# Linear attention's opening pass: TensorE turns the decayed keys ahead of the modulation chunk's matmuls, state sums ahead of the chunk's group sum

## The chip, the cores and the metric

One NeuronCore of a Trainium2 chip runs the whole program. The metric is the device time in microseconds (us) of one execution; the number given for a kernel is the median of its runs. The engines are TensorE (PE; PEld is its weight load), VectorE (DVE), ScalarE (ACT), GpSimd (POOL) and SyncE (SP), which here only issues DMA transfers. Each engine works through its own instructions in the order in which they are written, and a wait on a semaphore at the head of an engine's queue holds everything behind it on that engine.

## The reference

The program computes one transformer layer for 128 context tokens and 1024 latent tokens. Two parts of it meet in the stretch that is changed. The first is the linear attention (4 heads, keys of 64 and values of 128), in chunks with a decay that depends on the data:

```
def step(S, xs):
    qc, kc, vc, gc = xs
    cum = jnp.cumsum(gc, axis=2)
    o_inter = jnp.einsum('bhik,bhkv->bhiv', qc * jnp.exp(cum), S)
...
    last = cum[:, :, -1:, :]
    S = (jnp.exp(last[:, :, 0, :])[..., None] * S
         + jnp.einsum('bhjk,bhjv->bhkv', kc * jnp.exp(last - cum), vc))
```

It runs once forward and once backward over the tokens. The second is the modulation, a vector of 6 x 1024 numbers for each of the two conditioning vectors:

```
m = (jax.nn.silu(cond) @ w_ada + b_ada)[:, None, :]
sh1, sc1, g1, sh2, sc2, g2 = jnp.split(m, 6, axis=-1)
h = rms_norm(x, norm_mix) * (1 + sc1) + sh1
...
x = x + g1 * mo
h = rms_norm(x, norm_ffn) * (1 + sc2) + sh2
x = x + g2 * moe_ffn(h, *ffn_p)
```

Only `sh1` and `sc1` are needed before the token mixer. The other four parts, 4096 columns of `w_ada`, are computed beside the linear attention. Attention, the output projection and a mixture of 32 experts follow.

## The kernel before

The program is a row of stages (`with stage(...)`), written with an explicit queue for each engine and explicit semaphores. A stage ends with all engines meeting before the next begins. The changed code is in the second stage, which holds the linear attention. In the trace of before it runs from about 358 us to about 478 us.

There are nine tiles of 128 tokens (`NT` = 9: one of context, eight latent), taken in the order of `FIRST` in an opening pass, and in the order of `SECOND` in a closing pass that makes the outputs. The opening pass is one loop on every engine, with `i` from 0 to 8. For tile i:

- PE `gates(i)` (L920, 4 products) makes the gate's pre-activations, five tiles ahead.
- ACT `size` (L704, L705) and `log` (L709) turn them into logarithms of decays. `log` needs another function table, so an ACT_TABLE_LOAD stands ahead of each block of `log`, and another ahead of the next `grow`. Two `size` come after `grow(0)` and `grow(3)`; one `size` and three `log` come after `grow(1)` and `grow(4)`.
- DVE `decay(i)` (L819 to L833) scans them into cumulated decays.
- ACT `grow(i)` (L716, L718, L719) takes exponentials; its first instruction, L716, makes `ek`.
- DVE `decay_keys(i)` (L838) multiplies the keys with `ek` and signals `kf_made`.
- PE `turn(i)` (L929) transposes the decayed keys into PSUM bank 2. ACT `keep_turned(i)` (L724) copies them out as `kTM` and signals `kTM_made`.
- PE `sums(i)` (L939) multiplies them with the values: the tile's contribution to the state. DVE `add(i)` (L844) scales it, and `step` (L854) carries the states from tile to tile.

Mixed into the same loop, for `i` from 0 to 7 (`NADA` = 8), is one chunk of 512 modulation columns:

- SP `load(n)` (L657) fetches 2 MB of `w_ada` into one of two buffers `RING_B`. From chunk 2 on it waits for `ada_parted` of chunk n-2, which used the buffer. `row_out(n-2)` (L670) and `rows(n)` (L662) follow on SP, and wait for `mod2_ready`. For n = 5, SP also waits for the fifth `mod2_ready` before it reloads `nrow2` (L666); `load(6)` is queued behind that.
- PE `ada_part(n)` (L949) makes four groups of partial products in PSUM bank 6, and ACT `ada_keep(n)` (L732) copies them to SBUF and signals `part_kept`.
- PE `ada_sum(n)` (L957) adds the groups and the bias into bank 7. ACT `ada_row(n)` (L740) copies out the row and signals `mod2_ready`; for n = 4 and 5, DVE `ada_scaled(n)` (L861) does so in its place.

On ACT the loop's body is, in this order, `grow(i)`, any `size` and `log`, the three copies, and then `grow(i+1)`. On DVE it is `decay(i+1)`, `decay_keys(i)`, `add(i-1)`, `step(i-3)`, and `ada_scaled(i-1)` for the two chunks named. After the loop DVE goes through `mask(0)`, the last `add` and the remaining `step`, and then the closing pass.

Of the kernel before, what the change touches and what calls it, by code (L numbers as in the profile page):

```python
# [36 lines left out]
def trunk_kernel(nc, t_in, t_out):  # L37
# [52 lines left out]
    with ctx:  # L90
# [5 lines left out]
        def sem(name):  # L96
            if name not in sems:
                sems[name] = nc.alloc_semaphore(name=f"{name}_{stages[0]}")
            return sems[name]
# [183 lines left out]
        def bank(b, n=H, off=0):  # L283
            return PS[:, b * H + off:b * H + off + n]
# [346 lines left out]
        NADA = 8  # L631
# [11 lines left out]
        with stage("pads_out cache_in") as block:  # L643
# [54 lines left out]
            @block.scalar  # L698
            def _(act):
                own = Chain(act, sem("own_gla_act"))  # L700

                def size(i):
                    act.wait_ge(sem("z_made"), i + 1)
                    own.link(nc.scalar.activation(u4(ag[i]), u4(bank(z_bank(i))), ACT.Abs))  # L704
                    nc.scalar.activation(ag[i], ag[i], ACT.Exp, scale=-1.0).then_inc(sem("z_exp"), 1)  # L705

                def log(i):
                    act.wait_ge(sem("z_exp"), i + 1)
                    nc.scalar.activation(ag[i], ag[i], ACT.Ln, bias=1.0).then_inc(sem("ln_made"), 1)  # L709

                def grow(i):
                    g = FIRST[i]
                    act.wait_ge(sem("decay_made"), i + 1)
                    if i >= 2:
                        act.wait_ge(sem("kf_made"), i - 1)
                    nc.scalar.activation(ek[i % 2], Dt[i % 2], ACT.Exp, scale=-1.0 / 16).then_inc(sem("ek_made"), 1)  # L716
                    act.wait_ge(sem("qf_made"), i)
                    nc.scalar.activation(eq, Dt[i % 2], ACT.Exp, scale=1.0 / 16).then_inc(sem("eq_made"), 1)  # L718
                    nc.scalar.activation(vecs[:, :, :, g], vecs[:, :, :, g], ACT.Exp, scale=1.0 / 16).then_inc(sem("vecs_made"), 1)  # L719

                def keep_turned(i):
                    act.wait_ge(sem("kf_turned"), i + 1)
                    act.wait_ge(sem("sums_made"), i)
                    nc.scalar.activation(kTM, bank(2), ACT.Copy).then_inc(sem("kTM_made"), 1)  # L724

                def ada_keep(n):
                    act.wait_ge(sem("ada_parted"), n + 1)
                    if n >= 2:
                        act.wait_ge(sem("ada_summed"), n - 1)
                    else:  # L730
                        act.wait_ge(sem("part2_cleared"), 1)
                    nc.scalar.activation(part2[n % 2][0:BIAS_ROW], bank(6)[0:BIAS_ROW], ACT.Copy).then_inc(sem("part_kept"), 1)  # L732

                def ada_row(n):
                    if n in (4, 5):
                        return
                    act.wait_ge(sem("ada_summed"), n + 1)
                    if n >= 2:
                        act.wait_ge(sem(f"rows_out{n % 2}"), 16 * (n // 2))
                    nc.scalar.activation(mrow2[n % 2], bank(7)[0:2, :], ACT.Copy).then_inc(sem("mod2_ready"), 1)  # L740

                def square(s):
                    act.wait_ge(sem("gla_made"), s + 1)
                    act.wait_ge(sem("o_mean"), s)
                    for h in range(GH):
                        last = nc.scalar.activation(osq[:, h * P:(h + 1) * P], bank(o_bank(s) + h % 2, P, h // 2 * P), ACT.Square, accum_out=so4[:, h:h + 1])
                    last.then_inc(sem("o_squared"), 1)

                for i in range(3):
                    size(i)  # L750
                for i in range(3):
                    log(i)
                for i in range(NT):
                    grow(i)
                    if i + 3 < NT and i % 3 == 0:
                        size(i + 3)
                        size(i + 4)
                    if i + 4 < NT and i % 3 == 1:
                        size(i + 4)
                        for k in range(i + 2, i + 5):  # L760
                            log(k)
                    if i < NADA:
                        ada_keep(i)
                    keep_turned(i)
                    if i < NADA:
                        ada_row(i)
                for s in range(NT):
                    square(s)
# [143 lines left out]
            def _(pe):  # L912
                pe.wait_ge(sem("gate_w_in"), 64)

                def gates(i):
                    g = FIRST[i]
                    if i >= 4:
                        pe.wait_ge(sem("decay_logged"), i - 3)
                    for u in range(4):
                        last = nc.tensor.matmul(bank(z_bank(i), P, u * P), WG[u // 2][:, (u % 2) * P:(u % 2 + 1) * P], lrT1[:, g * P:(g + 1) * P],  # L920
                                                start=True, stop=True)
                    last.then_inc(sem("z_made"), 1)

                def turn(i):
                    g = FIRST[i]
                    pe.wait_ge(sem("kf_made"), i + 1)
                    pe.wait_ge(sem("kTM_made"), i)
                    for u in range(4):
                        last = nc.tensor.transpose(bank(2, P, u * P), kf[:, g, u * P:(u + 1) * P], ident)  # L929
                    last.then_inc(sem("kf_turned"), 1)  # L930

                def sums(i):
                    g = FIRST[i]
                    pe.wait_ge(sem("kTM_made"), i + 1)
                    pe.wait_ge(sem("added"), i)
                    for u in range(4):
                        for half in range(2):
                            h = 2 * (u % 2) + half
                            last = nc.tensor.matmul(bank(3, P, u * P)[64 * half:64 * half + 64], kTM[:, u * P + 64 * half:u * P + 64 * half + 64],  # L939
                                                    v_all[:, g, h * DV:(h + 1) * DV], start=True, stop=True)  # L940
                    last.then_inc(sem("sums_made"), 1)

                def ada_part(n):
                    pe.wait_ge(sem(f"ada2_in{n % 2}"), 16 * (n // 2 + 1))
                    pe.wait_ge(sem("part_kept"), n)
                    for jj in range(2):
                        for r in range(4):
                            j = 2 * r + jj
                            last = nc.tensor.matmul(bank(6)[32 * r:32 * r + 32], scP[:, j * 32:(j + 1) * 32], RING_B[n % 2][:, j, :],  # L949
                                                    start=(jj == 0), stop=(jj == 1))  # L950
                    last.then_inc(sem("ada_parted"), 1)

                def ada_sum(n):
                    pe.wait_ge(sem("part_kept"), n + 1)
                    pe.wait_ge(sem(f"brow2_in{n % 2}"), 16 * (n // 2 + 1))
                    pe.wait_ge(sem("mod2_ready"), n)
                    nc.tensor.matmul(bank(7)[0:2, :], sel, part2[n % 2], start=True, stop=True).then_inc(sem("ada_summed"), 1)  # L957

                def score(s):
                    g = SECOND[s]  # L960
                    pe.wait_ge(sem("qf_made"), FIRST.index(g) + 1)
                    pe.wait_ge(sem("gla_masked"), 2 * s)
                    for u in range(4):
                        for half in range(2):
                            rows = slice(64 * half, 64 * half + 64)
                            last = nc.tensor.matmul(bank(half, P, u * P), kf[rows, g, u * P:(u + 1) * P], qkT[rows, u, g * P:(g + 1) * P],
                                                    start=True, stop=True)
                    last.then_inc(sem("gla_scored"), 1)
# [25 lines left out]
                for i in range(NT):  # L994
                    if i + 5 < NT:
                        gates(i + 5)
                    if i < NADA:
                        ada_part(i)
                    if i == NT - 1:
                        score(0)  # L1000
                    turn(i)
                    if i < NADA:
                        ada_sum(i)
                    sums(i)
                for s in range(NT):
                    if s + 1 < NT:
                        score(s + 1)
# [1164 lines left out]
```

## Time and profile before

| | before |
|---|---|
| runs, us | 2623.21, 2623.43, 2631.17 |
| median, us | 2623.43 |
| profiled execution: time, us | 2625.44 |
| profiled execution: span, us | 2623.8 |
| PE busy | 2393.7 us, 91% |
| DVE busy | 1545.6 us, 59% |
| ACT busy | 1337.5 us, 51% |
| granted TensorE clock, mean | 0.965 |

The span is the time from the first to the last instruction of the profiled execution, and the execution's own time is 1.6 us longer. The busy shares are those of the whole program, most of which is the mixture of experts. For a change in a single stage the rows of that stage are to be read, by time. A granted clock of 1.00 is TensorE at 2.4 GHz, and 0.50 is 1.2 GHz.

### The profile page before, as it was taken

The numbers are of one execution on the slowest core, as the hardware profiler recorded it, in microseconds if no ns is written. First come the engines' busy times: TensorE is split into PE (matmuls) and PEld (weight loads), VectorE is DVE, ScalarE is ACT, GpSimd is POOL, SyncE is SP. The second block draws the span as 40 slices with busy tenths as digits, with TensorE's granted clock in tenths as the row PEclk, the third lists the DMA queues.
The fourth block names the chain that finished last, engine by engine and source line by source line (L and its number), as shares of the span: only waits on it lengthen the run. The fifth ranks groups of instructions, "written<-read, shape, count | busy, mean of one in ns | idle before, by whom it ended". The sixth has DMA issues, their size and how long they took to land.

```text
span 2623.8 us, 55140 instructions
## 1 busy us (share of the span) xinstructions
PE 2393.7 (91%) x19125; PEld 1346.1 (51%) x19126; DVE 1545.6 (59%) x1828; ACT 1337.5 (51%) x1395; POOL 831.7 (32%) x946
## 2 busy tenths in 40 slices
PE   6999987799989959899899998889988999999991
PEld 2555555577755535455455554445544555545550
DVE  2222247566636675953934659999689624175975
ACT  1111143366532345843834658888588524165861
POOL 1222223500003353433333443434334433233322
PEclk9999989999999979999999999999999999999995
DMA  8000043420032286964945869999899835177974
GB/s 322 21 18 18 9 155 124 136 81 0 0 130 82 99 291 221 396 237 130 362 169 164 284 240 361 398 396 394 292 343 397 300 87 169 28 276 264 359 278 177
DMA packets 180248, 538.48 MB, mean 205 GB/s; under 512 B 20672, under 2 KB 37490, under 8 KB 180142
## 3 DMA queue, kind: packets, MB, share of 16 engines
q1 hardware_dynamic: 150620, 487.79, 49.0%
q0 software_dynamic: 26656, 46.85, 8.1%
q10 hardware_dynamic: 2916, 3.14, 0.4%
q8 instruction: 30, 0.49, 0.1%
q14 instruction: 26, 0.21, 0.0%
HBM read 493.11 MB, written 45.20 MB: 205 GB/s over the span
## 4 chain that ended last, share of the span: by engine, by line
PE 55%; DVE 6%; issue 5%; DMA 2%; ACT 2%; POOL 0%; ACTq 0%; DVEq 0%; POOLq 0%; SPq 0%
PE psum L2065 44%; PE psum L1968 5%; DVE arena L1836 4%; PE psum L2054 2%; PE psum L2049 2%; DMA arena<-in_w_down 1%; PE psum L2043 1%; ACT arena L1657 1%; PE psum L1984 1%; DMA expert_lists<-arena 0%; DVE arena L1930 0%; DVE arena L1931 0%; PE psum L1977 0%; DVE arena L1944 0%; DVE arena L1895 0%
## 5 line engine op out<-in xcount | busy, mean ns | idle before, releaser
L2065 PE MATMUL psum<-arena 128*64 128x512 bf16 x12528 | 1422.9, 383 | 66.6 <-DVE arena L1885 36.0
L2065 PEld LDWEIGHTS psum<-arena 128*64 128x64 bf16 x12528 | 717.5, 111 | 721.8 <-DVE arena L1836 49.6
L1836 DVE TENSOR_TENSOR arena<-arena 128x2048 bf16<-128x2048 f32 x384 | 862.7, 2287 | 184.9 <-ACT arena L1657 177.9
L1657 ACT ACTIVATE arena<-arena 128x2048 bf16<-128x2048 f32 x384 | 723.2, 1904 | 94.9 <-DVE arena L1836 64.9
L1566 POOL DMA_INDIRECT expert_sums<-arena x90 | 185.7, 2064 | 671.6 <-issue 649.7
L555 PE MATMUL psum<-arena 128*128 128x512 f32 (+2 forms) x864 | 298.9, 505 | 1.1 <-ACT arena L411 1.1
L555 PEld LDWEIGHTS psum<-arena 128*128 128x128 f32 x864 | 151.0, 191 | 133.6 <-issue 129.0
L1885 DVE TENSOR_TENSOR arena<-psum,arena 128x512 bf16<-128x512 f32 x87 | 59.8, 688 | 234.3 <-ACT arena L1699 234.3
L1537 POOL DMA_INDIRECT arena<-expert_inputs,arena x88 | 108.2, 1230 | 198.4 <-PE psum L2043 178.5
L1695 ACT ACTIVATE arena<-psum 128x1024 bf16<-128x1024 bf16 x87 | 88.5, 1017 | 156.4 <-issue 153.8
L1710 ACT ACTIVATE arena<-psum,arena 128x512 f32<-128x512 f32 x87 | 59.3, 681 | 201.0 <-PE psum L2065 201.0
L1968 PE MATMUL psum<-arena 128*128 128x512 f32 x288 | 129.7, 605 | 1.4 <-DVE arena L1766 1.4
L1699 ACT ACTIVATE arena<-psum 128x512 bf16<-128x512 f32 x87 | 51.5, 592 | 155.8 <-PE psum L2049 155.6
L1895 DVE TENSOR_SCALAR arena<-psum 128x512 f32<-128x512 f32 x87 | 59.8, 687 | 111.1 <-PE psum L2065 111.1
L1588 POOL COPY arena<-arena 128x2 int32<-128x2 int32 x86 | 124.7, 1450 | 0.0
L1575 POOL DMA_DIRECT2D arena<-expert_lists x172 | 97.7, 585 | 51.7 <-issue 50.7
L1126 ACT ACTIVATE arena<-psum 128x512 f32<-128x512 f32 x104 | 58.0, 595 | 97.5 <-PE psum L1256 97.5
L2054 PE MATMUL psum<-arena 128*64 128x512 bf16 x522 | 103.1, 391 | 3.9 <-issue 3.4
L1256 PE MATMUL psum<-arena 128*128 128x128 f32 x640 | 92.1, 283 | 13.1 <-ACT arena L1126 8.2
L1553 POOL COPY arena<-arena 128x6 f32<-128x6 f32 x90 | 76.0, 845 | 83.6 <-DMA expert_sums<-arena 83.6
L1155 DVE TENSOR_REDUCE arena<-psum 128x1 f32<-128x512 f32 (+1 forms) x96 | 54.7, 599 | 64.2 <-PE psum L1219 64.2
L1106 ACT ACTIVATE arena<-psum,arena 128x1280 f32<-128x1280 f32 x64 | 84.9, 1327 | 7.2 <-DVE arena L1159 1.7
(268 smaller groups left out, 2161.5 us busy)
## 6 DMA issues: line engine op xcount, KB each, us to landing
arena<-in_w_gu SPq DMA_DIRECT2D x256, 1024.0 KB, 18.4
arena<-in_w_down SPq DMA_DIRECT2D x128, 1024.0 KB
arena<-in_w_ada SPq DMA_DIRECT2D x12, 2048.0 KB, 9.0
arena<-in_x_sample SPq DMA_DIRECT2D x16, 512.0 KB, 3.6
arena<-in_w_in SPq DMA_DIRECT2D x3, 2048.0 KB, 19.6
expert_sums<-arena SPq DMA_DIRECT2D x10, 512.0 KB, 6.1
expert_inputs<-arena SPq DMA_DIRECT2D x10, 512.0 KB, 2.8
x_after_mixing<-arena SPq DMA_DIRECT2D x9, 512.0 KB, 2.7
```

The costliest lines, as they stand in the source:

```text
L555: last = nc.tensor.matmul(bank(bk, n, off), hT[b][:, j * P:(j + 1) * P], w_in[:, j, lo:lo + n], start=(j == 0), stop=(j == KT - 1))
L1256: last = nc.tensor.transpose(bank(t_bank(r - 1, i), P, at * P), pr[(r - 1) % 2][:, v * KEYS + k * P:v * KEYS + (k + 1) * P], ident)
L1537: pool.indirect_dma_start(out=xg, out_offset=None, in_=h2_d, in_offset=bass.IndirectOffsetOnAxis(ap=present.bitcast(U32)[:, 0:1], axis=0)) ...
L1566: pool.indirect_dma_start(out=moe_halves, out_offset=bass.IndirectOffsetOnAxis(ap=held.bitcast(U32)[:, 2 * DELAY:2 * DELAY + 1], axis=0), ...
L1575: pool.dma_start(listed[group(h), :], pairs[:, h, :]).then_inc(sem("listed_in"), 16)
L1588: nc.gpsimd.tensor_copy(present, listed).then_inc(sem("present_kept"), 1)
L1657: nc.scalar.activation(high(e, p, c), raw[p][c], ACT.Copy).then_inc(sem(f"hi_made{c}"), 1)
L1695: nc.scalar.activation(xT, bank(B_X).bitcast(BF), ACT.Copy).then_inc(sem("xT_made"), 1)
L1836: nc.vector.tensor_tensor(w_lo[p][c], raw[p][c], high(e, p, c), ALU.subtract).then_inc(sem(f"lo_made{c}"), 1)
L1968: last = nc.tensor.matmul(bank(a), mixT[b][:, j * P:(j + 1) * P], w_out[:, j, a * H:(a + 1) * H], start=(j == 0), stop=(j == KT - 1))
L2054: nc.tensor.matmul(bank(b)[group(g)], pickrow[:, (first + g) * UNIT:(first + g + 1) * UNIT], rows, start=True, stop=False)
L2065: last = nc.tensor.matmul(bank(b)[group(g)], parts[part][:, cols], w[:, kk, g * H:(g + 1) * H], start=False, stop=(k == KT - 1 and part == 1))
```

## The change

Two pairs of calls change places in PE's loop, and one pair on ACT. On PE, `turn(i)` now stands ahead of `ada_part(i)`, and `sums(i)` ahead of `ada_sum(i)`. On ACT, `keep_turned(i)` stands ahead of `ada_keep(i)`. No instruction is added or removed, and no wait is changed.

```diff
@@ -759,10 +759,9 @@
                         size(i + 4)
                         for k in range(i + 2, i + 5):
                             log(k)
+                    keep_turned(i)
                     if i < NADA:
                         ada_keep(i)
-                    keep_turned(i)
-                    if i < NADA:
                         ada_row(i)
                 for s in range(NT):
                     square(s)
@@ -994,14 +993,14 @@
                 for i in range(NT):
                     if i + 5 < NT:
                         gates(i + 5)
-                    if i < NADA:
-                        ada_part(i)
                     if i == NT - 1:
                         score(0)
                     turn(i)
                     if i < NADA:
+                        ada_part(i)
+                    sums(i)
+                    if i < NADA:
                         ada_sum(i)
-                    sums(i)
                 for s in range(NT):
                     if s + 1 < NT:
                         score(s + 1)
```

On PE, in the iteration i = 2 of the opening pass, the rows of before read as follows. L920 is `gates`, L949 `ada_part`, L929 `turn`, L957 `ada_sum` and L939 `sums`; the brackets hold the semaphores that the instruction waits for, and `kf_made` comes from DVE's `decay_keys`.

```order
L920 MATMUL psum<-arena 128x128 [waits decay_logged_1]
L920 MATMUL psum<-arena 128x128 x3
L949 MATMUL psum<-arena 32x512 [waits part_kept_1,ada2_in0_1]
L949 MATMUL psum<-arena 32x512 x7
L929 MATMUL psum<-arena 128x128 [waits kTM_made_1,kf_made_1]
L929 MATMUL psum<-arena 128x128 x3
L957 MATMUL psum<-arena 2x512 [waits mod2_ready_1,brow2_in0_1,part_kept_1]
L939 MATMUL psum<-arena 64x128 [waits added_1,kTM_made_1]
L939 MATMUL psum<-arena 64x128 x7
```

In the change the same iteration reads as follows. The line numbers of PE's functions are one lower there: L928 is `turn`, L948 `ada_part`, L938 `sums` and L956 `ada_sum`.

```order
L919 MATMUL psum<-arena 128x128 [waits decay_logged_1]
L919 MATMUL psum<-arena 128x128 x3
L928 MATMUL psum<-arena 128x128 [waits kTM_made_1,kf_made_1]
L928 MATMUL psum<-arena 128x128 x3
L948 MATMUL psum<-arena 32x512 [waits part_kept_1,ada2_in0_1]
L948 MATMUL psum<-arena 32x512 x7
L938 MATMUL psum<-arena 64x128 [waits added_1,kTM_made_1]
L938 MATMUL psum<-arena 64x128 x7
L956 MATMUL psum<-arena 2x512 [waits mod2_ready_1,brow2_in0_1,part_kept_1]
```

The wait for `kf_made` now stands ahead of the eight products of `ada_part`, and `ada_sum` is the last of the iteration.

On ACT, the end of the same iteration and the start of the next read as follows before. L732 is `ada_keep`, L724 `keep_turned`, L740 `ada_row`, and L716 the first instruction of the next `grow`.

```order
L732 ACTIVATE arena<-psum 98x512 [waits ada_summed_1,ada_parted_1]
L724 ACTIVATE arena<-psum 128x512 [waits sums_made_1,kf_turned_1]
L740 ACTIVATE arena<-psum 2x512 [waits rows_out0_1,ada_summed_1]
L716 ACTIVATE arena<-arena 128x512 [waits kf_made_1,decay_made_1]
L718 ACTIVATE arena<-arena 128x512 [waits qf_made_1]
```

In the change they read:

```order
L724 ACTIVATE arena<-psum 128x512 [waits sums_made_1,kf_turned_1]
L732 ACTIVATE arena<-psum 98x512 [waits ada_summed_1,ada_parted_1]
L740 ACTIVATE arena<-psum 2x512 [waits rows_out0_1,ada_summed_1]
L716 ACTIVATE arena<-arena 128x512 [waits kf_made_1,decay_made_1]
L718 ACTIVATE arena<-arena 128x512 [waits qf_made_1]
```

The two copies have changed places; the row's copy L740 still stands ahead of the next `grow`, and still waits for `ada_sum`.

## Rows read from the trace of the kernel before

**Rows 1.** The page's chain that ended last, by line, share of the span.

```profile
PE psum L2065 44%; PE psum L1968 5%; DVE arena L1836 4%; PE psum L2054 2%; PE psum L2049 2%; DMA arena<-in_w_down 1%; PE psum L2043 1%; ACT arena L1657 1%; PE psum L1984 1%; DMA expert_lists<-arena 0%; DVE arena L1930 0%; DVE arena L1931 0%; PE psum L1977 0%; DVE arena L1944 0%; DVE arena L1895 0%
```

**Rows 2.** Windows: us, PE, PEld, DVE, ACT, POOL busy (x), PEclk, DMA share, GB/s.

```profile
372.40:428.00 55.60, 44.63 (x331) 18.62 (x332) 41.81 (x104) 34.90 (x65) 12.48 (x16) 0.87 0.74 262
428.07:438.50 10.43, 8.81 (x106) 7.73 (x106) 10.39 (x28) 2.35 (x11) 2.77 (x4) 1.00 0.00 0
```

**Rows 3.** Timeline of DVE: start, duration; all of `decay_keys` but i = 6.

```profile
373.04 0.68 DVE L838 TENSOR_TENSOR arena<-arena 128x512 f32<-128x512 f32 x1
...
378.93 0.69 DVE L838 TENSOR_TENSOR arena<-arena 128x512 f32<-128x512 f32 x1 [1.26 <-ACT arena L716]
...
387.80 0.69 DVE L838 TENSOR_TENSOR arena<-arena 128x512 f32<-128x512 f32 x1 [1.59 <-ACT arena L716]
...
392.78 0.68 DVE L838 TENSOR_TENSOR arena<-arena 128x512 f32<-128x512 f32 x1
...
398.69 0.69 DVE L838 TENSOR_TENSOR arena<-arena 128x512 f32<-128x512 f32 x1
...
405.44 0.69 DVE L838 TENSOR_TENSOR arena<-arena 128x512 f32<-128x512 f32 x1 [0.39 <-ACT arena L716]
...
423.46 0.69 DVE L838 TENSOR_TENSOR arena<-arena 128x512 f32<-128x512 f32 x1 [4.96 <-ACT arena L716]
...
428.07 0.69 DVE L838 TENSOR_TENSOR arena<-arena 128x512 f32<-128x512 f32 x1 [2.08 <-ACT arena L716]
```

**Rows 4.** Timeline of PE, iteration i = 2.

```profile
386.16 1.16 PE L920 MATMUL psum<-arena 33*128 33x128 f32 x8
387.24 1.92 PE L949 MATMUL psum<-arena 128*32 128x512 f32 x16
389.10 0.66 PE L929 MATMUL psum<-arena 128*128 128x128 f32 x4
389.88 1.02 PE L957 MATMUL psum<-arena 128*2 128x512 f32 x2
390.83 1.09 PE L939 MATMUL psum<-arena 128*64 128x128 f32 x16
```

**Rows 5.** Timeline of ACT, end of iteration i = 2.

```profile
389.23 0.60 ACT L732 ACTIVATE arena<-psum 98x512 f32<-98x512 f32 x1 [0.83 <-PE psum L949]
...
390.94 0.59 ACT L740 ACTIVATE arena<-psum 2x512 f32<-2x512 f32 x1 [0.55 <-PE psum L957]
391.43 0.61 ACT L716 ACTIVATE arena<-arena 128x512 f32<-128x512 f32 x1
```

**Rows 6.** Timeline of PE: the waits of i = 1, 4 and 6.

```profile
384.18 1.02 PE L957 MATMUL psum<-arena 128*2 128x512 f32 x2 [1.88 <-ACT arena L732]
...
403.03 1.29 PE L957 MATMUL psum<-arena 128*2 128x512 f32 x2 [2.40 <-ACT arena L732]
404.26 1.98 PE L939 MATMUL psum<-arena 128*64 128x128 f32 x16
...
416.91 3.64 PE L949 MATMUL psum<-arena 128*32 128x512 f32 x16 [5.63 <-DMA arena<-in_w_ada]
```

**Rows 7.** Timeline of ACT: around the blocks of `log`, i = 1 and 4.

```profile
383.56 0.57 ACT L732 ACTIVATE arena<-psum 98x512 f32<-98x512 f32 x1
...
385.84 1.28 ACT L716 ACT_TABLE_LOAD   x1
...
397.13 0.61 ACT L716 ACTIVATE arena<-arena 128x512 f32<-128x512 f32 x1
...
404.78 0.63 ACT L716 ACTIVATE arena<-arena 128x512 f32<-128x512 f32 x1
```

**Rows 8.** Timeline of DVE and of SP: `ada_scaled(4)`, and the issue of `load(6)`.

```profile
407.89 0.67 DVE L861 SCALAR_TENSOR_TENSOR arena<-psum,arena 2x512 f32<-2x512 f32 x1
...
408.87 0.39 SPq L657 DMA_DIRECT2D arena<-in_w_ada  x1
```

**Rows 9.** Windows, with the granted clock: behind the waits of 1.88 and 2.40 us.

```profile
382.00:385.00 3.00, 1.12 (x5) 0.15 (x3) 2.29 (x3) 2.62 (x5) 0.00 (x0) 1.00 1.00 313
403.00:406.00 3.00, 2.97 (x18) 1.66 (x18) 2.54 (x10) 2.97 (x5) 0.00 (x0) 0.61 0.04 14
```

## Prediction

> **What bounds the kernel now.** I read the page's chain first: over half of the span hangs on the experts' matmuls, which the change doesn't touch [rows 1]. So its worth has to be read from the stage of the linear attention, and passed on one to one: all engines meet at the stage's end, and nothing of the next stage starts ahead of that.
>
> The windows come next. In the opening pass, 55.60 us long, PE is busy for 44.63, DVE for 41.81 and ACT for 34.90: no engine is full, so the pass is held by chains between them. In the 10.43 us behind it DVE is busy for 10.39 [rows 2]. That stretch is one unbroken run of DVE from `decay_keys(8)` to its last `step`, and the closing pass hangs on it. **So what the change does to the time is what it does to the start of `decay_keys(8)`.**
>
> The timeline of DVE gives the beat of the pass, the starts of `decay_keys` [rows 3]. From i = 0 to 5 the steps are 5.89, 8.87, 4.98, 5.91 and 6.75 us, from i = 5 to 7 it is 18.02, and from 7 to 8 it is 4.61. Where a row of it has a wait, it is for ACT's L716, the exponential.
>
> What sets the beat before? Chunk i's row is a loop of its own: `ada_part(i)`, `ada_sum(i)`, ACT `ada_row(i)`, the next `grow`, `decay_keys(i+1)`. But `ada_part(i+1)` doesn't wait for `decay_keys(i+1)`; it runs while ACT and DVE make the keys. In iteration 2, `ada_part` runs from 387.24 to 389.16, and `decay_keys(2)` from 387.80 to 388.49: the keys are ready before `turn` gets to them, and cost PE nothing [rows 3, 4].
>
> PE has three waits of note: 1.88 and 2.40 us for ACT's copy in iterations 1 and 4, where ACT is still at its `log`, and 5.63 us for `load(6)` [rows 6]. That load is issued at 408.87, right behind `ada_scaled(4)`, which ends at 408.56, and its data let PE go at 416.91, 8.04 us later [rows 6, 8].
>
> **The change part by part.** It moves work and adds none: 8 `ada_part`, 9 `turn`, 9 `sums`, 8 `ada_sum`, 17 copies. SP's list stays as it is, with its waits; what it waits for moves.
>
> *What is won.* The three waits above are partly filled: `sums` now covers the wait for `ada_keep`, `ada_part` that for `keep_turned`. This gives PE room, but the beat isn't set by PE's room.
>
> *What is lost.* `turn(i)` waits for `decay_keys(i)`, and now `ada_part(i)` is behind it. `ada_sum(i)` is behind `sums(i)`, and ACT's next `grow` still waits for `ada_row(i)`, which waits for `ada_sum(i)`. The two loops close into one: keys, turn, part, sums, group sum, row, exponential, keys. At full clock, start to start or with a handover of 0.05 us (L716 to L732 show such):
> - `decay_keys` 0.68 and a handover 0.05: 0.73 [rows 3]
> - `turn` 0.66 [rows 4]
> - `ada_part` 387.24 to 389.10: 1.86 [rows 4]
> - `sums` 1.09, taken as 1.04 to the next start; `ada_sum` 1.02 and a handover: 1.06 [rows 4]
> - `ada_row` 390.94 to 391.43: 0.49; L716 0.61 and a handover: 0.66 [rows 5]
>
> That is 6.50 us. Now each step against [rows 3]:
> - **2 to 3:** 6.50 for 4.98, +1.5.
> - **3 to 4:** 6.50, and 0.25 since two `size` of 1.15 us each hold up `keep_turned(3)` until just after `ada_part(3)`. 6.75 for 5.91, +0.8.
> - **7 to 8:** 6.50 for 4.61, +1.9.
> - **0 to 1:** PE is at half clock when it begins. `ada_part` takes 3.64 there, as a slow one does [rows 6], in place of 1.86: 8.3 for 5.89, +2.4. If the clock rises within that `ada_part` it is +1.3; if `sums` is slow as well (1.98 [rows 6]), +3.3.
> - **1 to 2:** ACT's `log` sets it. Its copies can start at 383.56 as before [rows 7]; now `keep_turned` is first (0.60 and a handover), then come `sums` 1.04, `ada_sum` 1.06, `ada_row` 0.49, the table 1.28 [rows 7], and L716 0.66. That leads to 388.74 in place of 387.80: +0.9.
> - **4 to 5:** ACT alone sets it, from `grow(4)` at 397.13 to `grow(5)` at 404.78, 7.65 us [rows 7], since no `ada_row(4)` is on ACT. Before, `decay_keys(4)` came late by DVE's own work and the step was 6.75: +0.9.
> - **5 to 7:** `load(6)` is issued 3.43 us after `decay_keys(5)` starts, on DVE's work alone, and takes its 8.04 [rows 3, 6, 8]. From `ada_part(6)` to `decay_keys(7)` it was 6.55 [rows 3, 6]; now it is 3.57 at half clock, and 1.04, 1.06, 0.49, 0.66: 6.8. +0.3, or +1.1 with a slow `sums`. The wait of 5.63 doesn't absorb what was lost earlier, as the load's issue is late by the same amount.
>
> The sum is 1.5 + 0.8 + 1.9 + 2.4 + 0.9 + 0.9 + 0.3 = **+8.7 us** at full clock in the middle of the pass.
>
> *The clock.* PE now idles ahead of nearly each `turn`. From the end of `ada_sum(i-1)` it is 0.05 + 0.49 + 0.66 + 0.73, 1.9 us, to `turn(i)`: all of it idle in iterations 4, 6 and 7, less 1.1 us of `gates` [rows 4] in 1 to 3, and 1.28 more for the table in iteration 2, 2.1 us. The rows of before bound what such a wait does: behind 1.88 us the granted clock was 1.00, behind 2.40 us it was 0.61, and the next `sums` took 1.98 instead of 1.09 [rows 4, 6, 9]. The new waits of about 2 us lie in between. An iteration at half clock costs 3.64 - 1.92 in `ada_part` and 1.98 - 1.09 in `sums`, 2.6 us, where the loop sets the step (2 to 3, 3 to 4, 7 to 8). I take one half of one such iteration, 1.3 us: **+10.0 us.** The Trainium skill, in "TensorE: Matmul & The Clock Gate", section "A second HAM failure mode: psum-queue depth-cycling", tells of a kernel whose short idle times between groups of matmuls make the clock go back and forth between its two levels. By that rule all three of these iterations would be slow, and the sum would be that of the second rival below; the trace so far agrees only for the wait of 2.40 us.
>
> **The rivals.**
> 1. *The loop closes through `ada_part`* (the forecast): +8 to +13 us. Chance 0.65.
> 2. *The same, and the clock stays down.* The three steps lose 2.6 us each, 0 to 1 is at its 3.3, 5 to 7 at its 1.1: 8.7 + 7.8 + 0.9 + 0.8 = +18 us. Against it: PE is busy for more of a slow iteration than of a fast one, and in before the granted clock had a mean of 0.87 over the pass with its waits of 2.40 and 5.63 us in it [rows 2, 6]. Chance 0.12, from +13 up.
> 3. *The pass is held by the modulation weights, and early losses vanish in PE's wait for `load(6)`* (no change). For it: 5.63 us of wait, the longest in the pass. Then only what comes behind counts, 0.3 + 1.9 = +2 us. It decides if `ada_scaled(4)` isn't late, that is if `decay_keys(5)` isn't. Against it: the steps to there add up to 6.5. A partial form, in which the clock rises early and some steps lose less, ends near +7. Chance 0.20 for both.
> 4. *Faster: the room on PE is what counts.* If ACT's next `grow` gained from the earlier `keep_turned`, and PE's waits of 1.88, 2.40 and 5.63 us all vanished, the pass would be 9.9 us shorter. It takes a `grow` that isn't behind `ada_row`; the order on ACT speaks against it. Chance 0.03.
>
> **How the numbers follow.** The profiled span of 2623.8 would become 2633.8, and its own time of 2625.44 would be 2635.4; the median lies 2.0 below that time, so 2623.43 + 10.0 = 2633.4. From no change a measurement here tells about 0.3%, 7.9 us (2631.3). The forecast and rival 2 lie above that, rival 3 below, rival 4 at the other side: slower 0.77, same 0.20, faster 0.03. The range for 8 in 10 goes from +6 (the partial form of rival 3) to +16.5 (most of rival 2): 2629.5 to 2640.
>
> **What would show it.** In the trace after, PE's `turn` should have waits for DVE's keys in iterations 0 to 7, of 1 to 2 us, and no wait for ACT's `ada_keep`. The beat of `decay_keys` should be 6.5 us from 2 to 3 and from 7 to 8. `load(6)` should be issued some 6.5 to 9 us later than 408.87, and PE should still wait for it, some 3 us. `decay_keys(8)` should start near 438, and the rest of the program keep its lengths. I am wrong if `ada_part` comes through at its old times although it is behind `turn`, or if the later stages shift by more than the pass; and wrong in size if the clock takes another way than above.

## The result and the profile after

The changed kernel takes 2641.52 us (median of 6 runs, 2639.14 to 2647.64), beside 2626.76 us for the kernel before (6 runs, 2623.21 to 2631.17). The ratio is 1.0061, with a 95% interval of 1.0049 to 1.0072: slower by 13 to 19 us. Timed again on another occasion (the run `after_again`) it was 2642.29 us beside 2628.24 us, a ratio of 1.0040 (1.0025 to 1.0056), or 7 to 15 us. The ratios are estimates with intervals of their own; the plain quotients of the medians are 1.0056 and 1.0053, inside both. The forecast was 2633.4 us, in a range of 2629.5 to 2640.0: the direction was right, and the time lies above the range.

The beat of the pass comes first, as in [rows 3]. In the changed kernel `decay_keys` has line L837. These are rows of DVE's timeline (start, duration, operation, and in brackets the idle time ahead and what ended it):

```profile
376.06 0.68 DVE L837 TENSOR_TENSOR arena<-arena 128x512 f32<-128x512 f32 x1
385.00 0.69 DVE L837 TENSOR_TENSOR arena<-arena 128x512 f32<-128x512 f32 x1 [4.32 <-ACT arena L716]
394.89 0.69 DVE L837 TENSOR_TENSOR arena<-arena 128x512 f32<-128x512 f32 x1 [2.63 <-ACT arena L716]
402.94 0.69 DVE L837 TENSOR_TENSOR arena<-arena 128x512 f32<-128x512 f32 x1 [2.98 <-ACT arena L716]
409.58 0.69 DVE L837 TENSOR_TENSOR arena<-arena 128x512 f32<-128x512 f32 x1 [0.65 <-ACT arena L716]
417.24 0.69 DVE L837 TENSOR_TENSOR arena<-arena 128x512 f32<-128x512 f32 x1 [0.39 <-ACT arena L716]
423.74 0.68 DVE L837 TENSOR_TENSOR arena<-arena 128x512 f32<-128x512 f32 x1
435.94 0.69 DVE L837 TENSOR_TENSOR arena<-arena 128x512 f32<-128x512 f32 x1 [5.63 <-ACT arena L716]
443.98 0.69 DVE L837 TENSOR_TENSOR arena<-arena 128x512 f32<-128x512 f32 x1 [5.52 <-ACT arena L716]
```

From the first to the ninth it is 67.92 us, where it was 55.03 us in [rows 3]: **+12.9 us**. Below, "the pass" always means this stretch. DVE now waits for ACT's exponential in seven of the nine rows, twice for over 5 us.

What follows the pass kept its lengths. From the ninth `decay_keys` to TensorE's first instruction of the next stage it is 50.14 us (50.13 before), and from there to the end of the span 2145.5 us (2145.6). What lies ahead did not: the stage begins 2.9 us later than in the trace of before, at 360.91 instead of 358.05, in code that the change doesn't touch. 12.9 and 2.9 are the 15.8 us between the two spans, 2639.6 and 2623.8.

Iteration 2 on TensorE, beside [rows 4]; L928 is `turn`, L948 `ada_part`, L938 `sums`, L956 `ada_sum`:

```profile
395.64 0.95 PE L928 MATMUL psum<-arena 128*128 128x128 f32 x4 [2.26 <-DVE arena L837]
396.52 3.26 PE L948 MATMUL psum<-arena 128*32 128x512 f32 x16
399.72 1.09 PE L938 MATMUL psum<-arena 128*64 128x128 f32 x16
400.74 1.02 PE L956 MATMUL psum<-arena 128*2 128x512 f32 x2
```

And ACT in the same iteration, beside [rows 5], with SyncE's issue of `load(6)`, beside [rows 8]:

```profile
399.86 0.60 ACT L732 ACTIVATE arena<-psum 98x512 f32<-98x512 f32 x1 [2.63 <-PE psum L948]
401.80 0.59 ACT L740 ACTIVATE arena<-psum 2x512 f32<-2x512 f32 x1 [1.34 <-PE psum L956]
...
420.66 0.39 SPq L657 DMA_DIRECT2D arena<-in_w_ada  x1
```

The reader is to see the order of time. `decay_keys(2)` starts at 394.89; `turn` waits for it; `ada_part`, `sums` and `ada_sum` follow in one block; ACT's row copy waits for `ada_sum` at 401.80; and `decay_keys(3)` starts at 402.94. One thing is behind the other all the way round. `ada_part` takes 3.26 us where it took 1.92 [rows 4], since the clock fell right behind the wait of 2.26 us. The windows show it (us, PE, PEld, DVE, ACT and POOL busy, granted clock, DMA share, GB/s): iteration 2 from `turn` to the end of `ada_part`, and the wait and the work of iteration 7. The clock is still 1.00 while TensorE waits, and 0.56 in the work behind.

```profile
395.60:399.70 4.10, 4.06 (x20) 1.15 (x20) 4.00 (x9) 0.60 (x1) 1.46 (x2) 0.58 0.22 53
434.00:436.60 2.60, 0.76 (x2) 0.00 (x0) 0.66 (x2) 1.74 (x4) 0.00 (x0) 1.00 0.02 4
437.00:440.70 3.70, 3.70 (x20) 0.90 (x18) 1.45 (x3) 0.60 (x1) 1.23 (x2) 0.56 0.00 0
```

### The profile page after: what moved, and what is told of

Its sections match the earlier page's. It is cut to its first block, busy times and chain, and to the rows that moved or that the text cites. A ratio compares the mean times of both kernels' runs of the same rounds, so it can differ in the third digit from the quotient of the medians.

```text
span 2639.6 us, 55140 instructions
## 1 busy us (share of the span) xinstructions
PE 2396.2 (91%) x19125; PEld 1344.7 (51%) x19126; DVE 1546.0 (59%) x1828; ACT 1337.6 (51%) x1395; POOL 833.6 (32%) x946
## 4 chain that ended last, share of the span: by engine, by line
PE 53%; DVE 6%; issue 5%; DMA 3%; ACT 2%; POOL 1%; ACTq 0%; DVEq 0%; SPq 0%; POOLq 0%
PE psum L2064 42%; PE psum L1967 5%; DVE arena L1835 4%; DMA arena<-in_w_down 2%; PE psum L2053 2%; PE psum L2048 2%; PE psum L2042 1%; ACT arena L1656 1%; PE psum L1983 1%; DVE arena L1929 0%; DMA expert_lists<-arena 0%; DVE arena L1894 0%; DVE arena L1930 0%; PE psum L1976 0%; DVE arena L1943 0%
```

## The experiments

Theory A is that of the prediction, with the clock as the miss in size. The rivals that were tried against it: B, all of the loss is the place of `sums`; C, all of it is `turn`'s wait ahead of `ada_part`; D, the clock is the larger part of the loss, or, for the long steps, none of it. Each kernel's pass is read from its own trace.

| kernel | pass, us | steps 2 to 3 / 5 to 7 / 7 to 8, us | ratio to before (95%) |
|---|---|---|---|
| before; again | 55.03; 54.84 | 4.98 / 18.02 / 4.61 | |
| change; again | 67.92; 68.97 | 8.05 / 18.70 / 8.04 | 1.0061; 1.0040 |
| `e9_scalar_only` | 62.35 | 5.32 / 19.36 / 5.66 | 1.0043 (1.0027 to 1.0059) |
| `e1_turn_only` | 63.21 | 7.42 / 17.97 / 6.17 | 1.0034 (1.0023 to 1.0044) |
| `e2_sums_only` | 64.50 | 5.31 / 19.46 / 5.31 | 1.0043 (1.0028 to 1.0057) |
| `e3_row_later` | 55.60 | 4.99 / 16.17 / 5.33 | 0.9998 (0.9989 to 1.0006) |
| `e4_filled` | 77.89 | 10.20 / 25.42 / 8.74 | 1.0097 (1.0082 to 1.0111) |
| `e5_filled_less` | 64.48 | 8.64 / 16.46 / 6.41 | 1.0035 (1.0023 to 1.0048) |
| `e6_before_load6` | 49.43 | 4.99 / 13.25 / 3.81 | 0.9973 (0.9963 to 0.9984) |
| `e8_both` | 48.93 | 4.99 / 12.98 / 2.58 | 0.9969 (0.9956 to 0.9982) |
| `e7_after_load6` | 60.89 | 8.05 / 13.00 / 6.40 | 1.0025 (1.0013 to 1.0036) |

### Parts of the change

**`e1_turn_only`**: the change, without the second pair on TensorE.

```diff
                     turn(i)
                     if i < NADA:
                         ada_part(i)
-                    sums(i)
-                    if i < NADA:
                         ada_sum(i)
+                    sums(i)
```

> The change without its second half on TensorE: turn is ahead of ada_part, but ada_sum is ahead of sums, as before; ScalarE as in the change. The pass, from the start of the first decay_keys to that of the ninth, was 55.0 us before and 67.9 us after. Theory A (one loop through keys, turn, part, group sum, row, exponential; sums' place in it adds 1.04 us per step where the loop sets the beat): steps 2 to 3 and 7 to 8 of about 5.5 us at full clock (6.3 with the ScalarE copy waited for), 8 with a clock that is down; the pass 61 to 64 us. Rival B (all of the loss is the place of sums, which delays ada_sum): the pass 55 to 56 us. Rival C (all of the loss is turn's wait ahead of ada_part): the pass stays at 67 to 68 us.

**`e2_sums_only`**: the kernel before, with this pair alone.

```diff
                     turn(i)
+                    sums(i)
                     if i < NADA:
                         ada_sum(i)
-                    sums(i)
```

> The second half alone: ada_part ahead of turn and the two copies on ScalarE as before, but sums ahead of ada_sum. Theory A: the row's loop has keep_turned, sums and ada_sum in it behind ada_part and turn (0.66 + 0.6 + 0.6 + 1.04 + 1.06), and the block of log delays sums(1) and sums(4), which ada_sum now waits behind: the pass 62 to 65 us. Rival B (the place of sums is all): 67 to 68 us. Rival C (turn's wait is all): 55 to 56 us.

**`e9_scalar_only`**: the kernel before, with the pair on ScalarE alone.

```diff
+                    keep_turned(i)
                     if i < NADA:
                         ada_keep(i)
-                    keep_turned(i)
-                    if i < NADA:
                         ada_row(i)
```

> The part of the change on ScalarE alone: keep_turned ahead of ada_keep, TensorE's order as before. Theory A: ada_keep, and with it ada_sum, ada_row and the next exponential, now wait for turn and its copy (0.66 + 0.6 us), 0.7 to 1.3 us for each step in which the row's loop sets the beat, more with a slow clock: the pass 59 to 64 us in place of 55.0. If the order of the two copies is neutral by itself, the pass is 55 to 56 us.

Measured, the passes are 63.2, 64.5 and 62.4 us, all in theory A's ranges, and B and C both fall: each of the three versions costs 7 to 9.5 us, and the whole costs 12.9. (The move of `turn` was tried only together with the ScalarE pair, never by itself.) They don't add up; theory A's reason is that each lengthens the same path, the one to `ada_row`. By these traces, one of each, the ScalarE pair alone is already +7.3 us; with it in place `turn`'s move adds only 0.9 (62.4 to 63.2), and that of `sums` 4.7 more. Iteration 2 of `e9_scalar_only` shows the path, TensorE first, then ACT:

```profile
390.54 1.92 PE L948 MATMUL psum<-arena 128*32 128x512 f32 x16
392.40 0.65 PE L928 MATMUL psum<-arena 128*128 128x128 f32 x4
394.23 1.02 PE L956 MATMUL psum<-arena 128*2 128x512 f32 x2 [1.18 <-ACT arena L732]
...
393.09 0.60 ACT L724 ACTIVATE arena<-psum 128x512 f32<-128x512 f32 x1 [1.38 <-PE psum L928]
393.58 0.59 ACT L732 ACTIVATE arena<-psum 98x512 f32<-98x512 f32 x1
395.28 0.59 ACT L740 ACTIVATE arena<-psum 2x512 f32<-2x512 f32 x1 [1.11 <-PE psum L956]
395.78 0.61 ACT L716 ACTIVATE arena<-arena 128x512 f32<-128x512 f32 x1
```

`ada_part` ends at 392.46, but `ada_keep` (L732) can't go ahead of `keep_turned` (L724), which waits for `turn`. It starts at 393.58, TensorE idles for 1.18 us for it, and row and exponential follow. In the kernel before, `ada_keep` started 0.07 us after `ada_part` ended [rows 4, 5]. Iteration 2 shows the path, but little of the cost: its step is 5.32 us in place of 4.98. In `e9_scalar_only` the largest loss is in the step 0 to 1, 8.24 us in place of 5.89, where TensorE is at half clock; in `e2_sums_only` it is in the step 1 to 2, 11.79 in place of 8.87, where `sums(1)` waits for 3.39 us for `keep_turned(1)` behind ACT's `log`, and `ada_sum(1)` is behind it.

### The path to the row cut

**`e3_row_later`**: the change, but ScalarE issues `ada_row(i)` behind `grow(i+1)`.

```diff
                 for i in range(NT):
                     grow(i)
+                    if 1 <= i <= NADA:
+                        ada_row(i - 1)
...
                     keep_turned(i)
                     if i < NADA:
                         ada_keep(i)
-                        ada_row(i)
```

> The change as it is on TensorE, but ScalarE's ada_row(i) is issued behind grow(i+1), so that the next exponential doesn't wait for the group sum. Theory A says that the loop closes only through ada_row: cut there, the loop is keys, turn, part, ada_keep, exponential, 4.5 us, below VectorE's own work of about 6 us per tile; the steps 2 to 3 and 7 to 8 fall to 4.6 to 4.9 us and the pass to 54 to 56 us, the time to within 3 us of the kernel before (the kernel before has ada_row ahead). Rival C (turn's wait ahead of ada_part costs by itself, by late weights and late group sums): the pass stays above 62 us. Rival D (the clock is the larger part of the loss): the pass falls by 4 us at most, since turn still waits.

Measured: the pass is 55.60 us and the ratio 0.9998 (0.9989 to 1.0006). All three swaps of the change are still in, and the loss is gone from the total. The steps 2 to 3 and 7 to 8 are 4.99 and 5.33 us, a little above the 4.6 to 4.9 expected. Iteration 2 on TensorE and on ACT:

```profile
389.12 0.66 PE L929 MATMUL psum<-arena 128*128 128x128 f32 x4
389.70 1.92 PE L949 MATMUL psum<-arena 128*32 128x512 f32 x16
391.56 1.09 PE L939 MATMUL psum<-arena 128*64 128x128 f32 x16
392.58 1.02 PE L957 MATMUL psum<-arena 128*2 128x512 f32 x2
...
391.70 0.60 ACT L732 ACTIVATE arena<-psum 98x512 f32<-98x512 f32 x1 [1.29 <-PE psum L949]
392.19 0.62 ACT L716 ACTIVATE arena<-arena 128x512 f32<-128x512 f32 x1
```

The exponential L716 starts at 392.19, before `ada_sum` does (392.58), and `turn` has no wait. So 12.3 of the 12.9 us need the exponential to be queued behind the row, and rival C, which had the pass stay above 62 us, falls. D in its first form had the pass fall by 4 us at most, and is wrong in that; but the run doesn't part the clock from the loop, since with the loop go most of the waits behind which the clock fell.

The new order isn't free even so. `e8_both`, below, has the row behind the exponential too, but the old order of everything else, and its `load(6)` is moved only later in the pass. Its first three `decay_keys` (L840) come sooner after one another than those of `e3_row_later` (L838), first the latter's:

```profile
372.69 0.68 DVE L838 TENSOR_TENSOR arena<-arena 128x512 f32<-128x512 f32 x1
379.33 0.69 DVE L838 TENSOR_TENSOR arena<-arena 128x512 f32<-128x512 f32 x1 [2.02 <-ACT arena L716]
388.37 0.69 DVE L838 TENSOR_TENSOR arena<-arena 128x512 f32<-128x512 f32 x1 [0.39 <-ACT arena L716]
...
372.82 0.68 DVE L840 TENSOR_TENSOR arena<-arena 128x512 f32<-128x512 f32 x1
377.71 0.69 DVE L840 TENSOR_TENSOR arena<-arena 128x512 f32<-128x512 f32 x1 [0.26 <-ACT arena L718]
385.84 0.69 DVE L840 TENSOR_TENSOR arena<-arena 128x512 f32<-128x512 f32 x1 [0.40 <-ACT arena L718]
```

That is 15.68 us against 13.02. Here `turn`'s wait ahead of `ada_part` does cost time, since `ada_keep` still stands ahead of the exponential: `ada_part(0)` starts 1.78 us behind `decay_keys(0)` in `e3_row_later`, and 0.66 us ahead of it in `e8_both`. Against the kernel before, `e3_row_later` loses in the steps 0 to 2 (+0.9), 4 to 5 (+0.8) and 7 to 8 (+0.7), and gains 1.85 us from 5 to 7, where the exponential no longer waits for the row. Its 55.60 us is a balance of the two, and the kernel before with the row moved alone was not run.

### The clock

**`e4_filled`** and **`e5_filled_less`**: the change, with products in TensorE's waits, whose result nobody reads.

```diff
+                def fill(n):
+                    for _ in range(n):
+                        nc.tensor.matmul(bank(7)[32:64, :], scP[:, 0:32], v_all[:, 0, :], start=True, stop=True)
...
+                    fill((0, 0, 7, 0, 6, 0, 6, 6, 0)[i])
                     turn(i)
                     if i < NADA:
+                        fill(12 if i == 6 else 0)
                         ada_part(i)
```

> The change with idle TensorE filled: 7 products of 128x32 by 128x512, whose result nobody reads, ahead of turn(2), 6 ahead of turn(4), turn(6) and turn(7), and 12 ahead of ada_part(6); one takes 0.24 us at full clock. They work in time in which TensorE waits. Theory A with the clock as the miss in size: the granted clock stays at 1.00 through iterations 2 and 7, steps 2 to 3 and 7 to 8 go from 8.05 and 8.04 us to about 6.5, step 6 to 7 loses 1 to 2 us, the pass goes from 67.9 to 62.5 to 64.5 us. Rival D (the loss in these two steps has another cause, such as slower weight loads or a late semaphore): the two steps stay near 8 us.

The measure of the filling was wrong: a lone product takes 0.86 us at full clock, in two passes of 0.43, where I had read 0.24 from `ada_part`, whose products run four side by side. The row is that ahead of `turn(2)`, 7 products in 6.20 us instead of the wait of 2.26 us:

```profile
391.76 6.20 PE L954 MATMUL psum<-arena 128*32 128x512 f32 x14
```

The pass grew to 77.9 us, and the run tells nothing on the size of the clock's share. In `e5_filled_less` the counts are 2 ahead of `turn(2)`, `turn(6)` and `turn(7)`, and 3 ahead of `ada_part(6)`:

> The change with idle TensorE filled to the right measure. The run before showed one such product to take 0.86 us and not 0.24, so here 2 stand ahead of turn(2), turn(6) and turn(7) (1.7 us, where TensorE waits for 1.9 to 2.3) and 3 ahead of ada_part(6) (2.6 us in a wait of 3.4). Theory A with the clock as the miss in size: granted clock 1.00 in iterations 2 and 7, steps 2 to 3 and 7 to 8 at 6.5 us in place of 8.05 and 8.04, the two steps from 5 to 7 at 16.5 to 17.3 in place of 18.7; the pass at 62.5 to 64 us in place of 67.9. Rival D (these steps are long for another reason): they stay near 8 us and the pass above 67.

Measured: the last step fell from 8.04 to 6.41 us, and the two from 5 to 7 from 18.70 to 16.46, as theory A had them (6.5, and 16.5 to 17.3). The step from 2 to 3 did not fall: 8.64 us. The windows say why (columns as above), first `gates` of iteration 2, then filling and `turn(2)`, then iteration 7:

```profile
391.00:393.40 2.40, 2.40 (x9) 1.78 (x8) 0.00 (x0) 1.84 (x2) 0.00 (x0) 0.50 1.05 407
393.40:397.00 3.60, 3.60 (x6) 0.55 (x5) 2.87 (x4) 1.29 (x4) 1.45 (x2) 0.50 0.50 142
434.00:440.00 6.00, 5.58 (x54) 2.75 (x54) 2.11 (x5) 2.53 (x6) 1.46 (x2) 1.00 0.01 4
```

Here the clock had fallen already behind the wait of `sums(1)` for ACT, 2.00 us, an iteration before the filling, and the two products took 3.62 us and held up `turn`. The pass, 64.5 us, ended just above what was expected (62.5 to 64). What the clock costs in this kernel is so shown for the last step, 1.6 us, and for the two from 5 to 7, 2.2 us, and not by itself for the step from 2 to 3. `e7_after_load6`, below, agrees on the last step: with `ada_part(7)` at its 1.92 us it is 6.40 us.

### The wait for the sixth load

**`e6_before_load6`**: the kernel before, with `load(6)` ahead of SyncE's wait for `ada_scaled(4)`. **`e7_after_load6`** is the same edit on the change, and **`e8_both`** is `e6_before_load6` with the edit on ScalarE of `e3_row_later`.

```diff
                     if n in (4, 5):
                         if n == 5:
+                            load(6)
                             sp.wait_ge(sem("mod2_ready"), 5)
...
                 for n in range(2, NADA):
-                    load(n)
+                    if n != 6:
+                        load(n)
```

> The kernel before, with one move on SyncE: load(6) is issued ahead of the wait for the fifth mod2_ready instead of behind it. In the kernel before TensorE waits 5.63 us for it. Theory A: the beat is then VectorE's from 5 to 7 (6.5 + 6.5 in place of 18.0) and the pass 49 to 51 us in place of 55.0, 4 to 6 us faster in all. Rival 3 of the prediction in its strong form (the pass is held by the weights' bandwidth): the load is issued earlier but lands late, TensorE still waits for over 2 us, and the pass is 53 us or more.

> The change, with load(6) issued ahead of SyncE's wait for the fifth mod2_ready. In the change TensorE waits 3.4 us for that load, and then starts at half clock. Theory A: the steps from 5 to 7 are 13 us in place of 18.7, the clock stays up in iteration 7 and the last step is 6.5 us in place of 8.0: the pass 60.5 to 63 us in place of 67.9 (and 69.0 in a second run). If the loop through turn holds these steps too, they stay above 15 us and the pass above 64.

> The kernel before, with load(6) issued early and with ada_row(i) behind grow(i+1) on ScalarE. Theory A: cutting the row's loop from the exponential gains a further 1 to 2 us in the first steps and the last, the pass is 46.5 to 49.5 us in place of 55.0, and the time 6 to 8 us below before. If the row's loop doesn't hold the beat of the kernel before at all, it comes out as the version with load(6) alone, 49 to 51 us.

Measured: 49.43, 60.89 and 48.93 us, all three in theory A's ranges. But `e8_both` is only 0.5 us below `e6_before_load6`, where a gain of 1 to 2 us was expected. `load(6)` in `e6_before_load6` is issued at 403.21, and TensorE's `ada_part(6)` starts at 414.80 with no wait for it:

```profile
403.21 0.39 SPq L657 DMA_DIRECT2D arena<-in_w_ada  x1
...
414.80 1.92 PE L951 MATMUL psum<-arena 128*32 128x512 f32 x16
```

So the weights' bandwidth doesn't hold the pass of the kernel before; the place of one wait in SyncE's list did. `e6_before_load6` is 0.27% faster than the kernel before (interval 0.16% to 0.37%), and `e8_both` 0.31% (0.18% to 0.44%); their intervals overlap, so which of the two is better is not told by them. Against `e6_before_load6`, `e8_both` gains 1.0, 0.7 and 1.2 us in the steps 0 to 1, 1 to 2 and 7 to 8, and loses 2.7 in one: the earlier exponentials bring TensorE to `ada_part(4)` ahead of its weights, and the step from 4 to 5 is 9.45 us in place of 6.75:

```profile
399.44 3.20 PE L951 MATMUL psum<-arena 128*32 128x512 f32 x16 [2.56 <-DMA arena<-in_w_ada]
```

This too is at least in part SyncE's list: `ada_part(2)` frees the buffer at 388.41, and `load(4)` is issued at 391.22, behind four transfers of new states (L687).

### Both kernels again

> The changed kernel once more, timed in more rounds beside the runs of the kernel before. If the part of the gap that lies ahead of the pass (2.9 us in the two profiles) is chance, the pass is again 66.5 to 69 us, the stretch ahead of it comes out anywhere within 3 us, and the ratio of the times is 1.0045 to 1.006, nearer to the 12.9 us that the pass loses. If the change costs something outside the pass as well, the ratio stays at 1.006 and more, and the stretch ahead of the pass or behind it is longer again.

> The kernel before once more, for a second trace. If its pass is as repeatable as the theory takes it to be, it is 55.0 us again within 1 us, while the stretch ahead of it and the closing pass may differ by up to 3 us with the granted clock.

The passes are 68.97 us (67.92) and 54.84 us (55.03), both as expected. The ratio of `after_again`, 1.0040, is below the expected 1.0045 to 1.006, so nothing speaks for a cost outside the pass. The second trace of before begins the stage at 360.77 us, as late as the changed kernel's first, with no change in it. The late start is in the first stage, whose projections ran more of their time at half clock. Before, before again, and after:

```profile
42.59 12.37 PE L555 MATMUL psum<-arena 128*128 128x512 f32 x48 [1.11 <-ACT arena L411]
```

```profile
43.61 14.07 PE L555 MATMUL psum<-arena 128*128 128x512 f32 x48 [1.11 <-ACT arena L411]
```

```profile
43.74 14.07 PE L555 MATMUL psum<-arena 128*128 128x512 f32 x48 [1.11 <-ACT arena L411]
```

The granted clock from 43.7 to 46.5 us is 1.00, 0.57 and 0.61. So of the 15.8 us between the first two spans, 12.9 belong to the change and 2.9 to chance. The closing pass varies as well: in the two traces of the change it is 50.14 and 51.51 us, and the rest behind it 2145.5 and 2147.7 us, with the same code.

## Why the prediction was right and wrong

**The path of the step.** "What the change does to the time is what it does to the start of `decay_keys(8)`" held: in the first two traces closing pass and rest are the same to 0.1 us.

**The loop.** The mechanism was right: the two loops close into one through `ada_row`. `e3_row_later` shows it for all but a small part, the keys' path to `ada_keep`. By steps, forecast at full clock and measured in the two traces:

| step | before | forecast | after; again |
|---|---|---|---|
| 0 to 1 | 5.89 | 8.3 | 8.94; 8.00 |
| 1 to 2 | 8.87 | 9.8 | 9.89; 10.67 |
| 2 to 3 | 4.98 | 6.5 | 8.05; 8.85 |
| 3 to 4 | 5.91 | 6.75 | 6.64; 6.64 |
| 4 to 5 | 6.75 | 7.65 | 7.66; 7.67 |
| 5 to 7 | 18.02 | 18.3 | 18.70; 19.09 |
| 7 to 8 | 4.61 | 6.5 | 8.04; 8.05 |

The steps in which the clock stayed up, 3 to 4 and 4 to 5, are within about 0.1 us of the sum of rows; `load(6)` was issued 3.42 us behind the start of `decay_keys(5)` (3.43 forecast), so late by the earlier losses, and TensorE still waited for it, 3.4 us, both as forecast.

**The step that failed** is the one on the clock: "I take one half of one such iteration, 1.3 us". The pass lost 12.9 us in one trace and 13.9 in the other, against 8.7 by the loop at full clock, so the slow clock took 4.2 to 5.2 us. It was down in iterations 2 and 7 of both traces, and longer than allowed for in 6 of both, in 0 of the first and in 1 of the second. The rows bear the difference out: in iteration 2 of the first trace `turn` and `ada_part` took 0.95 and 3.26 us instead of 0.66 and 1.92, 1.6 us more, and the step was 1.55 above its forecast; and `e5_filled_less` gets 1.6 us back in the last step and 2.2 in the two before it (of which 1.7 are the slow `ada_part(6)`, which the forecast had). The term per slow iteration was too large the other way (1.5 to 2.4 us measured, 2.6 forecast), since the clock comes back within the iteration.

The 1.3 stood on no row. The new waits ahead of `turn` lay between one that kept the clock (1.88 us) and one that didn't (2.40), and half of one iteration out of three was picked. The term also looked at these waits alone. "The three waits above are partly filled" was wrong for two of them: TensorE still waited for 2.00 us ahead of `sums(1)` and of `sums(4)`, for `keep_turned` behind ACT's `log`. In `after_again` the clock fell behind the first of these, as in `e5_filled_less`; `ada_sum(1)` and `gates` then took 1.80 and 2.08 us instead of 1.02 and 1.16:

```profile
388.49 1.09 PE L938 MATMUL psum<-arena 128*64 128x128 f32 x16 [1.99 <-ACT arena L724]
389.52 1.80 PE L956 MATMUL psum<-arena 128*2 128x512 f32 x2
391.25 2.08 PE L919 MATMUL psum<-arena 33*128 33x128 f32 x8
```

The section cited from the Trainium skill ("TensorE: Matmul & The Clock Gate", section "A second HAM failure mode: psum-queue depth-cycling", on a clock going back and forth under short idle times) was nearer to what the trace shows than my reading of the rows, though not all three iterations that it would have slowed were: iteration 3 stayed at full clock, and rival 2's +18 us did not come.

**The range** failed for a second reason, the base. It was laid around 2623.43 us, the median of three runs. Beside the change the kernel before had 2626.76 us, and in two later sets of 22 and 24 runs 2628.71 and 2628.24 us, with single runs from 2622 to 2635. Of the 8.1 us between forecast and result, 3.3 are the base of the same comparison, 2.9 the pass beyond its forecast +10.0, and the other 1.9 are within the scatter. The range had the bounds of the mechanism in it (+6 to +16.5), and nothing for the base: the difference of the medians, 14.8 us, lies inside these bounds, so it is the base that carries the time out of the range.

**The rivals.** Rival 3, the pass held by the weights, is wrong in its main form: the steps up to `decay_keys(5)` lost 8.8 us, and none of it vanished in the wait for `load(6)`. `e6_before_load6` takes that wait away by an earlier issue, and gains 5.6 us of pass. Its partial form, near +7, fell short as well; only in `after_again` was the step 0 to 1 shorter than forecast, 8.00 for 8.3, and later steps lost more. Rival 4 asked for a `grow` that isn't behind `ada_row`. `e3_row_later` is that, and is no faster than the kernel before: the exponential needs to be freed, but room on TensorE gains nothing.

## What to carry to other kernels

Before two calls change places in one engine's list, follow what stands last in the list to whoever waits for it: here the copy of the modulation row stood ahead of the next exponential on ScalarE, and harmless-looking swaps ahead of it made it late. When the tail of one chain is queued ahead of the head of another on an in-order engine, the two are one chain as soon as the tail is late. In the kernel before the row stood there too and its pass was 55.0 us, since the group sum came early; the swaps made the group sum late. Moving that tail (one line) won back nearly the whole loss, 12.3 of 12.9 us. And a forecast of some tenths of a per cent needs a base of more than three runs, and a clock term that is taken from several waits of the same length.

## What the hardware showed that was not expected

- A wait of one and the same length may or may not cost the clock. In the changed kernel TensorE waited for 1.92 us ahead of `turn(4)`, and `ada_part(4)` took 1.92 us; the same 1.92 us ahead of `turn(7)` was followed by an `ada_part(7)` of 3.19 us, with a granted clock of 0.56. In `e5_filled_less` the wait of 1.92 us ahead of `turn(4)` was followed by 3.55 us. In `e7_after_load6` 2.01 us ahead of `turn(7)` was followed by 1.92. In `e1_turn_only` even 2.37 us ahead of `ada_sum(1)` left the granted clock at 1.00 for the 5 us that followed; it fell only in `ada_part(2)` (3.11 us), behind a further wait of 1.24. What decides between them was not tried.
- Products with 32 output rows overlap when they go to different groups of rows: 16 passes of `ada_part` in 1.92 us, 0.12 each, where passes that all go to one group take 0.43 each. The Trainium skill says in "TensorEngine Tiling (Array Packing)", section "Tiling Modes", that tiles of 128x32 are four side by side and can work in parallel; the traces agree.
- The same code ahead of the stage took 355.9 to 361.3 us in thirteen traces of the eleven kernels. In the two compared above the whole 2.9 us are there by 58 us: 1.7 are the slower clock in the 48 products, and most of the rest is the same in the products just ahead (L582, eight of them in 4.75 us instead of 3.86). The spread of the other traces was not followed up.
